# Up matrix of the feed-forward network in seven block products of Strassen's kind, tokens in two passes, the residual kept in memory

## The chip, the cores and the metric

The kernel runs on one core of a Trainium2 chip. The metric is device microseconds of one execution, lower is better. Beside its time, one profiled execution is given: the profile lists every instruction of the engines TensorE (PE, with its weight loads as PEld), VectorE (DVE), ScalarE (ACT), GpSimd (POOL) and the queue of SyncE (SP), which here only issues DMAs.

## The reference

One decoder layer on 1024 prompt tokens and 64 sample tokens (1088 in all), model width 1024. The change lies in its last step, and all ahead of it (projection, selection, sparse attention, convolution) is as before.

```python
def mix_and_mlp(x, attn_o, conv_o, w_out, g_mix_post, g_mlp_pre, w_up, w_down, g_mlp_post):
    m = jnp.einsum('bte,ed->btd', jnp.concatenate([attn_o, conv_o], axis=-1), w_out)
    x = x + rmsnorm(m, g_mix_post)
    h = rmsnorm(x, g_mlp_pre)
    f = jnp.einsum('btf,fd->btd', jnp.square(jax.nn.relu(jnp.einsum('btd,df->btf', h, w_up))), w_down)
    return x + rmsnorm(f, g_mlp_post)
```

`w_up` is 1024 x 4096, `w_down` is 4096 x 1024, all float32.

## The kernel before

Everything below is in `phase_out_mlp`, the last phase; each engine has its program in the order of the code, and semaphores are the only link between engines. Precision comes from splitting: each float32 operand is a high part (rounded to the type fp32r) and a low part (the rest), and one product of two blocks is three matmuls, high x high, high x low, low x high (`product`, L2185 to L2187). So every operand, weights too, has to be made: ACT casts the high part (L2083 for weights, L2152 for the hidden values), POOL subtracts for the low part of weights (L2030), DVE for that of the hidden values (L2336).

First come nine tiles of rows of the output projection (`out_rows`, `turn_rows`), then the feed-forward network, in `NG` = 8 groups of 4 blocks of 128 hidden channels. A group has an up part of 12 blocks (4 channel blocks x 3 token chunks of 384, 384 and 320), each 8 x 3 matmuls into one PSUM bank, and a down part of 24 blocks (8 output blocks x 3 token chunks), each 4 x 3 matmuls, whose sums DVE adds to `acc0` and `moT` in SBUF (L2355). The matmuls of both parts are as wide as the chunk. Six banks go round. ACT takes the relu (L2160), DVE squares (L2343), ACT makes the high part and DVE the low part, and a block of the down part that needs the last hidden values comes behind others that don't. Weights come as eight slices of 128 x 1024 a group (`load`, 512 KB each); a slice is made high and low once and serves all 1088 tokens. Groups 1 to 6 are a loop. At the end `final_rows` turns the sums back to rows on PE, and ACT, POOL and DVE make the last norm; the input rows plus the first residual stay in SBUF (`x2`).

## Time and profile before

| | us |
|---|---|
| three runs | 1678.77, 1668.45, 1679.35 (median 1678.77) |
| the profiled execution | 1670.35, span 1668.6 |
| PE busy | 1536.3 (92%), mean granted clock 0.967 |
| DVE, ACT, POOL busy | 705.1, 612.4, 417.9 |

The span runs from the first to the last instruction; 1.75 us of the profiled time lie around it. A busy PE in such a table is one with a matmul in flight; how fast it goes is read from the distance between the starts of neighbouring matmuls.

### The profile page before, as it was taken

How to read it: one execution, taken by the hardware profiler on the slowest of the kernel's cores; microseconds unless marked ns; L12 is line 12 of the kernel's file. 1: busy time of each engine (PE TensorE's matmuls, PEld its weight loads, DVE VectorE, ACT ScalarE, POOL GpSimd, SP SyncE). 2: the span in 40 equal slices, each digit the busy share in tenths (PEclk: the TensorE clock that was granted, in tenths of full speed). 3: DMA queues.
4: the chain of work that ended last, by engine and by line, in shares of the span. 5: the costliest groups of instructions: out<-in, count | busy, mean ns of one | idle time of the engine just before them, and what ended most of it. 6: DMA issues, size and time to landing. Idle time of an engine off the chain costs nothing.

```text
span 1668.6 us, 22157 instructions
## 1 busy us (share of the span) xinstructions
PE 1536.3 (92%) x8544; PEld 1278.9 (77%) x8544; DVE 705.1 (42%) x1322; ACT 612.4 (37%) x1092; POOL 417.9 (25%) x432
## 2 busy tenths in 40 slices
PE   3798888998979999885999999999999999999995
PEld 2356625663468877454879999999999999999995
DVE  1234916777976544246454222222222222222224
ACT  3112725888325765474433112121212212030211
POOL 2132100112594221104332212121212121212124
PEclk9999998999989998997999999999999999999998
DMA  6011104143007000337001111111111111111112
GB/s 208 19 37 24 49 11 119 60 68 67 7 3 224 36 2 1 119 134 246 0 1 51 44 46 47 43 42 46 49 39 50 38 50 38 50 38 50 39 45 101
DMA packets 92884, 97.66 MB, mean 59 GB/s; under 512 B 14822, under 2 KB 80438, under 8 KB 90500
## 3 DMA queue, kind: packets, MB, share of 16 engines
q1 hardware_dynamic: 89324, 75.71, 15.5%
q0 software_dynamic: 3488, 20.98, 3.4%
q8 instruction: 46, 0.75, 0.2%
q14 instruction: 26, 0.21, 0.0%
HBM read 85.55 MB, written 11.45 MB: 58 GB/s over the span
## 4 chain that ended last, share of the span: by engine, by line
PE 51%; DVE 1%; POOL 1%; DMA 1%; issue 0%; ACT 0%; SPq 0%; DVEq 0%; POOLq 0%; ACTq 0%
PE ps L2185 17%; PE ps L2187 17%; PE ps L2186 17%; PE ps L2219 0%; POOL y L2069 0%; DVE wo L2291 0%; DVE y L2366 0%; DMA wo_raw<-in_w_out 0%; DMA out_y_p<-y 0%; POOL wlo L2030 0%; PE ps L2271 0%; DVE xlo L2282 0%; DVE wlo L2287 0%; DVE y L2376 0%; SPq L1979 0%
## 5 line engine op out<-in xcount | busy, mean ns | idle before, releaser
L2030 POOL TENSOR_TENSOR wlo<-wraw,whi 128x1024 fp32r<-128x1024 f32 x62 | 149.0, 2403 | 573.1 <-ACT whi L2083 573.1
L2186 PE MATMUL ps<-xlo,whi 128*128 128x384 f32 (+1 forms) x768 | 250.3, 326 | 0.0
L2185 PE MATMUL ps<-hhi,whi 128*128 128x384 f32 (+1 forms) x720 | 235.1, 327 | 0.8 <-POOL wlo L2030 0.8
L2187 PE MATMUL ps<-hhi,wlo 128*128 128x384 f32 (+1 forms) x720 | 235.2, 327 | 0.0
L2186 PE MATMUL ps<-hlo,whi 128*128 128x384 f32 (+1 forms) x720 | 234.9, 326 | 0.0
L2083 ACT CAST whi<-wraw 128x1024 fp32r<-128x1024 f32 x62 | 65.2, 1052 | 296.5 <-PE ps L2187 293.8
L2343 DVE TENSOR_TENSOR rel<-rel 128x384 f32<-128x384 f32 (+1 forms) x96 | 51.5, 537 | 283.6 <-ACT rel L2160 283.6
L2186 PEld LDWEIGHTS ps<-xlo,whi 128*128 128x128 f32 x768 | 144.2, 188 | 0.0
L2160 ACT ACTIVATE rel<-ps 128x384 f32<-128x384 f32 (+1 forms) x96 | 45.3, 473 | 264.3 <-PE ps L2187 264.3
L2185 PEld LDWEIGHTS ps<-hhi,whi 128*128 128x128 f32 x720 | 135.2, 188 | 1.1 <-POOL wlo L2030 1.1
L2187 PEld LDWEIGHTS ps<-hhi,wlo 128*128 128x128 f32 x720 | 135.2, 188 | 0.0
L2186 PEld LDWEIGHTS ps<-hlo,whi 128*128 128x128 f32 x720 | 135.1, 188 | 0.0
L1040 PE MATMUL ps<-hT,w 128*128 128x384 f32 (+1 forms) x384 | 120.3, 477 | 8.6 <-DMA w<-in_w_u 8.6
L2185 PE MATMUL ps<-xhiA,whi 128*128 128x384 f32 (+1 forms) x384 | 125.7, 327 | 0.8 <-POOL wlo L2030 0.8
L2187 PE MATMUL ps<-xhiA,wlo 128*128 128x384 f32 (+1 forms) x384 | 125.4, 327 | 0.0
L2187 PE MATMUL ps<-xhiC,wlo 128*128 128x384 f32 (+1 forms) x384 | 125.1, 326 | 0.0
L2185 PE MATMUL ps<-xhiC,whi 128*128 128x384 f32 (+1 forms) x384 | 125.1, 326 | 0.0
L1040 PEld LDWEIGHTS ps<-hT,w 128*128 128x128 f32 x384 | 74.1, 194 | 53.9 <-DMA w<-in_w_u 8.7
L1115 DVE TENSOR_SCALAR_CACHE_REDUCE mask<-moT,cand 128x384 bf16<-128x384 f32 (+3 forms) x132 | 109.0, 882 | 1.1
L473 PE MATMUL ps<-w,hT 128*128 128x328 f32 (+3 forms) x256 | 97.0, 534 | 0.0
L2355 DVE TENSOR_TENSOR moT<-ps,moT 128x384 f32<-128x384 f32 (+1 forms) x84 | 45.0, 535 | 119.8 <-PE ps L2187 119.7
L2355 DVE TENSOR_TENSOR acc<-ps,acc 128x384 f32<-128x384 f32 (+1 forms) x84 | 45.0, 535 | 113.7 <-PE ps L2187 112.8
(304 smaller groups left out, 2860.8 us busy)
## 6 DMA issues: line engine op xcount, KB each, us to landing
wraw<-in_w_up SPq DMA_DIRECT2D x32, 512.0 KB, 4.0
wraw<-in_w_down SPq DMA_DIRECT2D x32, 512.0 KB, 3.4
x<-in_x SPq DMA_DIRECT2D x16, 512.0 KB, 10.0
w<-in_w_rows SPq DMA_DIRECT2D x2, 2048.0 KB, 11.3
w<-in_w_u SPq DMA_DIRECT2D x2, 2048.0 KB, 10.5
wo_raw<-in_w_out SPq DMA_DIRECT2D x8, 512.0 KB, 6.2
out_y_p<-y SPq DMA_DIRECT2D x8, 512.0 KB, 2.6
up<-by_channel SPq DMA_DIRECT2D x32, 86.0 KB, 4.0
```

The source lines that it names most:

```text
L473: last = nc.tensor.matmul(bank[2 + u % 2][0:n, 0:w], hT[:, k, i * P:i * P + n], wslot[g % 2][:, k, 0:w], start=(k == 0), stop=(k == KC - 1))
L1040: last = nc.tensor.matmul(bank[2 + 2 * (q % 3) + half][:, 0:w], wslot[c // 2][:, k, col:col + P], hT[:, k, t0:t0 + w], start=(k == 0), sto ...
L1115: last = nc.vector.tensor_scalar(mk, sc, against[0:n, j:j + 1].bitcast(F32), None, op, ALU.add, accum_out=count[0:n, j:j + 1])
L2030: nc.gpsimd.tensor_tensor(wlo_of(j, last), raw[:], whi_of(j, last), ALU.subtract).then_inc(s_wlo, 1)
L2083: nc.scalar.copy(whi_of(j, last), raw[:]).then_inc(s_whi, 1)
L2160: nc.scalar.activation(rel[:, p % 3, 0:w], bank[b % NBK][:, 0:w], ACT.Relu).then_inc(s_re, 1)
L2185: nc.tensor.matmul(o, wh, xh, start=first, stop=False)
L2186: nc.tensor.matmul(o, wh, xl, start=False, stop=False)
L2187: return nc.tensor.matmul(o, wl, xh, start=False, stop=last)
L2343: nc.vector.tensor_tensor(rel[:, p % 3, 0:w], rel[:, p % 3, 0:w], rel[:, p % 3, 0:w], ALU.mult).then_inc(s_sq, 1)
L2355: nc.vector.tensor_tensor(dst, src, dst, ALU.add).then_inc(s_ad, 1)
```

## The change

All of it is in `phase_out_mlp` (and one weight tile, `uw4`, reserved in place of `xhiA`).

- The up matrix is worked in units of 256 hidden channels (two blocks of 128) against half of the model width (4 blocks of 128) twice, and against two halves of the tokens of a pass. That is a 2 x 2 by 2 x 2 block product, made with seven block products in place of eight (a form with shared sums: four sums of weight blocks, `sums`; four of input blocks, `x_t1` to `x_t4`; seven sums of results in PSUM, SBUF and DVE). A unit is 7 x 4 x 3 = 84 matmuls, each as wide as half of a pass.
- The tokens go in two passes, of 512 (halves of 256) and 576 (halves of 288): `both_passes` runs the eight groups twice. Weights are therefore loaded, split and summed twice, and what was made once for 1088 tokens is made for 512 and again for 576.
- The seven operands of a unit (`uw`, high and low) have one place each. `up_high` (ACT) and `up_low` (POOL) refill place i once PE has done product i of the unit before. The raw slice (`uraw`, now 1 MB) has one place too: `load_up` waits until all seven low parts of the unit before are made.
- `FBANK` gives each product its bank: products 0, 3 and 5 go on top of each other in bank 0, and ACT copies what stands there in between (`take`); 4 and 6 do so in bank 3. `sum_hidden` (DVE) makes the four hidden blocks from copies and banks, `squared` is relu and square in one.
- The down part has the form of before, with chunks of 512 in the first pass and 288 in the second (384 and 192 in its last group), on three banks. For its first three chunks PE does hidden blocks 0 to 2 and comes back for block 3.
- The rows x + residual go to DRAM (`rows_d`) and come back at the end. The rows of the first pass are finished in the first group of the second.
- Preparing the inputs of a pass is seven casts (`x_high`), seven subtractions (`x_low`) and four sums of 4 x 256 or 4 x 288 elements.

```diff
+    HALF_T = (256, 288)
...
+    FBANK = [0, 1, 2, 0, 3, 0, 3]
+    OPENS = (0, 1, 2, 4)
+    SUM_AT = {2: 4, 3: 2, 4: 3, 5: 1}
+    DBANK = [4, 5, 1]
...
+    def x_source(p, i):
+        return [block(p, 0, 0), block(p, 1, 0), block(p, 1, 1), block(p, 1, 1), block(p, 0, 1), block(p, 0, 0),
+                block(p, 1, 0)][i]
...
+    def w_source(i):
+        return [quarter(0, 0), quarter(0, 1), quarter(0, 1), wsum[:, 1, :, :], quarter(1, 0), wsum[:, 0, :, :],
+                quarter(1, 1)][i]
...
+    def both_passes(eng, body):
+        for p in range(2):
+            body(p, 0, True, False)
+            with eng.Fori(1, NG - 1) as g:
+                body(p, g, False, False)
+            body(p, NG - 1, False, True)
...
+            def load_up(g, j):
+                sp.dma_start(uraw[:].rearrange("p k h n -> p k (h n)"),
+                             up[:, :, bass.ds(g * (FG * P) + j * 2 * P, 2 * P)]).then_inc(s_ru, 16)
...
+            def body(p, g, first, last):
+                if not (p == 0 and first):
+                    sp.wait_ge(s_wlo, at(p, g, 1, NP))
+                    load_up(g, 1)
+                if not (p == 1 and last):
+                    sp.wait_ge(s_wlo, at(p, g, 1, NP) + NP)
+                    load_up(after(p, g, last)[1], 0)
...
+                else:
+                    up_low(p, g, 1, range(NP))
+
+                for d in range(2):
+                    down_low(p, g, d, last)
...
+                if more:
+                    up_low(*nxt, 0, (0, 1))
+                down_low(p, g, 2, last)
+                if more:
+                    up_low(*nxt, 0, (2, 3, 4))
+                down_low(p, g, 3, last)
+                if more:
+                    up_low(*nxt, 0, (5, 6))
...
+            def up_high(p, g, j, which, unit0=False):
+                for i in which:
+                    act.wait_ge(s_ru, at(p, g, j, 16) + 16)
+                    if i in SUM_AT:
+                        act.wait_ge(s_sum, at(p, g, j, 4) + SUM_AT[i])
+                    if not unit0:
+                        act.wait_ge(s_up, at(p, g, j, NP) - NP + i + 1)
+                    nc.scalar.copy(uw_of(i, 0), w_source(i)).then_inc(s_whi, 1)
...
+            def take(p, g, j, which, start):
+                hw, slot = HALF_T[p], {0: 0, 3: 1, 4: 2, 5: 0}[which]
+                act.wait_ge(s_up, at(p, g, j, NP) + which + 1)
+                if which == 5:
+                    act.wait_ge(s_add, at(p, g, j, 4) + 1)
+                elif not start:
+                    act.wait_ge(s_add, at(p, g, j, 4) - (0 if which == 3 else 1))
+                nc.scalar.copy(pb[:, slot, 0:hw], bank[FBANK[which]][:, 0:hw]).then_inc(s_cp, 1)
...
+                take(p, g, 0, 0, start)
...
+                up_high(p, g, 1, (0, 1, 2))
+                take(p, g, 0, 3, start)
+                up_high(p, g, 1, (3,))
...
+                take(p, g, 0, 4, start)
+                up_high(p, g, 1, (4,))
+                take(p, g, 0, 5, start)
...
+                up_high(p, g, 1, (5,))
+                hid_high(p, g, 0, 0)
+                up_high(p, g, 1, (6,))
+                hid_high(p, g, 0, 1)
+
+                take(p, g, 1, 0, False)
+                down_high(p, g, 0, last)
...
+            def unit(p, g, j, first, last_):
...
+                    if i == 5:
+                        pe.wait_ge(s_cp, N_CP + n4 + 2)
+                    if i == 6:
+                        pe.wait_ge(s_cp, N_CP + n4 + 3)
+                    for k in range(HK):
+                        s = slice(k * P, (k + 1) * P)
+                        last = product(bank[FBANK[i]][:, 0:hw], (uw[i][:, 0, s], uw[i][:, 1, s]),
+                                       (moving(p, i, 0)[:, k, :], moving(p, i, 1)[:, k, :]),
+                                       k == 0 and i in OPENS, k == HK - 1)
                     last.then_inc(s_up, 1)
...
+                        if q < 3:
+                            pe.wait_ge(s_hlo, N_HLO + grp(p, g, 4) + (4 if f == 3 else 3))
...
+                for q in range(3):
+                    part(q, range(FG - 1))
+                for q in range(3):
+                    part(q, range(FG - 1, FG))
+                for q in range(3, len(todo)):
+                    part(q, range(FG))
...
+            def sums(p, g, j):
+                n4 = at(p, g, j, 4)
+                dve.wait_ge(s_ru, at(p, g, j, 16) + 16)
+                nc.vector.tensor_tensor(wsum[:, 0, :, :], quarter(1, 0), quarter(1, 1), ALU.add).then_inc(s_sum, 1)
+                dve.wait_ge(s_sum, n4 + 1)
+                nc.vector.tensor_tensor(wsum[:, 1, :, :], wsum[:, 0, :, :], quarter(0, 0), ALU.subtract).then_inc(s_sum, 1)
+                nc.vector.tensor_tensor(quarter(1, 0), quarter(0, 0), quarter(1, 0), ALU.subtract).then_inc(s_sum, 1)
+                dve.wait_ge(s_sum, n4 + 2)
+                dve.wait_ge(s_wlo, at(p, g, j, NP) + 2)
+                nc.vector.tensor_tensor(quarter(0, 1), quarter(0, 1), wsum[:, 1, :, :], ALU.subtract).then_inc(s_sum, 1)
...
+            def sum_hidden(p, g, j, which):
+                n4, n7, hw = at(p, g, j, 4), at(p, g, j, NP), HALF_T[p]
+                b = lambda i: bank[i][:, 0:hw]
+                s = lambda i: pb[:, i, 0:hw]
+                if which == 0:
+                    dve.wait_ge(s_up, n7 + 2)
+                    dve.wait_ge(s_cp, N_CP + n4 + 1)
+                    o, x, y = ct[:, 0, 0, 0:hw], b(1), s(0)
+                elif which == 1:
+                    dve.wait_ge(s_cp, N_CP + n4 + 4)
+                    o, x, y = ct[:, 0, 1, 0:hw], b(2), s(0)
+                elif which == 2:
+                    o, x, y = ct[:, 1, 1, 0:hw], s(2), s(0)
+                else:
+                    dve.wait_ge(s_up, n7 + 7)
+                    o, x, y = ct[:, 1, 0, 0:hw], b(3), s(1)
+                nc.vector.tensor_tensor(o, x, y, ALU.add).then_inc(s_add, 1)
+            def squared(p, g, j, h):
+                dve.wait_ge(s_add, at(p, g, j, 4) + 2 * (h + 1))
+                o = ct[:, h, :, 0:HALF_T[p]]
+                nc.vector.scalar_tensor_tensor(out=o, in0=o, scalar=0.0, in1=o, op0=ALU.max,
+                                               op1=ALU.mult).then_inc(s_sq, 1)
+            def hid_low(p, g, j, h):
+                hw = HALF_T[p]
...
+                sum_hidden(p, g, 0, 1)
+                squared(p, g, 0, 0)
+                sum_hidden(p, g, 0, 2)
+                hid_low(p, g, 0, 0)
+                sum_hidden(p, g, 0, 3)
+                squared(p, g, 0, 1)
...
+                    if q == 0 and not late:
+                        sums(*after(p, g, last), 0)
```

**Two places in the order of instructions.** First ACT at the head of a group in the loop. Before:

```order
L2160 ACTIVATE rel<-ps 128x384 [waits o_hlo]
L2152 CAST hhi<-rel 128x384 [waits o_sq]
...
L2160 ACTIVATE rel<-ps 128x320 [waits o_hlo,o_up]
...
L2083 CAST whi<-wraw 128x1024 [waits o_up,o_raw0]
...
L2160 ACTIVATE rel<-ps 128x384 [waits o_hlo,o_up]
L2152 CAST hhi<-rel 128x320 [waits o_sq]
```

And after the change, in the loop of the first pass; `o_sum` is the semaphore of the weight sums on DVE, `o_ru` that of the raw slice, and the line L2327 is `take`:

```order
L2327 COPY moT<-ps 128x256 [waits o_add]
...
L2228 CAST uwA<-uraw 128x512 [waits o_up,o_ru]
...
L2228 CAST uwA<-uraw 128x512 [waits o_up]
...
L2227 REGISTER_ALU [waits o_sum]
L2228 CAST uwA<-uraw 128x512 [waits o_up]
...
L2327 COPY moT<-ps 128x256 [waits o_add,o_up]
```

The copy of product 3 now stands behind three casts of weights, the third of which waits for the fourth weight sum.

Second DVE at the end of the up part and the head of the down part. Before (the first group, whose sums are copied):

```order
L2343 TENSOR_TENSOR rel<-rel 128x320 [waits o_re]
L2336 TENSOR_TENSOR hlo<-rel,hhi 128x384 [waits o_hhi]
L2336 TENSOR_TENSOR hlo<-rel,hhi 128x320 [waits o_hhi]
L2353 COPY acc<-ps 128x384 [waits o_dn] x2
L2353 COPY acc<-ps 128x320 [waits o_dn]
```

After the change (`o_wf` counts the chunks of the down part that PE has done):

```order
L2672 TENSOR_TENSOR moT<-ps,moT 128x256 [waits o_ah]
L2678 SCALAR_TENSOR_TENSOR moT<-moT 128x2x256 [waits o_add]
L2672 TENSOR_TENSOR moT<-moT 128x256
...
L2685 TENSOR_TENSOR hlo<-moT,hhi 128x512 [waits o_oh]
...
L2760 TENSOR_TENSOR moT<-ps,moT 128x512 [waits o_wf]
...
L2591 TENSOR_TENSOR moT<-uraw 128x512 [waits o_ru]
...
L2593 TENSOR_TENSOR moT<-moT,uraw 128x512 [waits o_sum]
L2594 TENSOR_TENSOR uraw<-uraw 128x4x128
...
L2597 TENSOR_TENSOR uraw<-uraw,moT 128x4x128 [waits o_wlo]
...
L2760 TENSOR_TENSOR moT<-ps,moT 128x512 [waits o_wf] x2
```

Four weight sums for the next group now stand between the first and the second addition of the down part.

On POOL a group was eight subtractions of 128x1024; it is fourteen of 128x512 and four of 128x1024 now, in each of the two passes, with the last two of the four behind low parts of the next group's up weights.

## Rows read from the trace of the kernel before

**Rows 1.** The page: busy time of the engines (share of the span) and instructions.

```profile
PE 1536.3 (92%) x8544; PEld 1278.9 (77%) x8544; DVE 705.1 (42%) x1322; ACT 612.4 (37%) x1092; POOL 417.9 (25%) x432
```

**Rows 2.** Windows: stretch, length, busy us (count) of engines, granted clock, DMA share, GB/s.

```profile
1300.00:1400.00 100.00, 100.00 (x607) 100.00 (x606) 25.69 (x50) 19.24 (x34) 20.93 (x9) 1.00 0.16 47
```

**Rows 3.** Who waited for whom from 893 to 1640 us: total, times, longest.

```profile
POOL wlo L2030 <- ACT whi L2083: 566.4, 60, 14.0
ACT rel L2160 <- PE ps L2187: 264.3, 93, 3.7
```

**Rows 4.** Timeline of PE: starts at 512 and at 384 columns.

```profile
780.60 0.39 PE L2185 MATMUL ps<-wo,xhiC 128*128 128x512 f32 x1
...
796.24 0.39 PE L2185 MATMUL ps<-wo,xhiC 128*128 128x512 f32 x1
...
1002.07 0.33 PE L2185 MATMUL ps<-xhiA,whi 128*128 128x384 f32 x1
...
1008.66 0.33 PE L2187 MATMUL ps<-xhiC,wlo 128*128 128x384 f32 x1
```

**Rows 5.** Timeline of PE in the attention, narrower matmuls.

```profile
645.29 0.28 PE L1520 MATMUL ps<-keys,qS 128*128 128x256 f32 x1
645.41 0.49 PE L1530 MATMUL ps<-identf,kpT 128*128 128x128 f32 x3
...
665.78 0.30 PE L1519 MATMUL ps<-keys,qS 128*128 128x128 f32 x1
665.92 0.28 PE L1520 MATMUL ps<-keys,qS 128*128 128x128 f32 x1
```

**Rows 6.** Groups by shape from 745 us: count, busy us, mean ns, idle before.

```profile
L2160 ACT ACTIVATE rel<-ps 128x384 f32<-128x384 f32 x64 | 31.3, 491 | 181.8 <-PE ps L2187 181.8
L2127 ACT CAST xhiA<-moT 128x512 fp32r<-128x512 f32 x8 | 4.9, 616 | 0.0
L2083 ACT CAST whi<-wraw 128x1024 fp32r<-128x1024 f32 x62 | 65.2, 1052 | 296.5 <-PE ps L2187 293.8
L2355 DVE TENSOR_TENSOR acc<-ps,acc 128x384 f32<-128x384 f32 x56 | 31.2, 557 | 79.1 <-PE ps L2187 78.2
L1369 POOL TENSOR_TENSOR qS<-qT,qS 64x512 fp32r<-64x512 f32 x12 | 15.4, 1279 | 0.9
L2030 POOL TENSOR_TENSOR wlo<-wraw,whi 128x1024 fp32r<-128x1024 f32 x62 | 149.0, 2403 | 573.1 <-ACT whi L2083 573.1
```

**Rows 7.** Timeline of ACT, DVE and POOL: start, us, engine.

```profile
811.51 0.68 DVE L2287 TENSOR_TENSOR wlo<-moT,whi 128x512 fp32r<-128x512 f32 x1
811.67 2.77 POOL L2054 TENSOR_TENSOR x<-x,moT 128x1024 f32<-128x1024 f32 x1 [1.40 <-DVE moT L2319]
812.11 2.89 DVE L2329 TENSOR_TENSOR xlo<-moT,xhiA 128x512 fp32r<-128x512 f32 x1
...
885.21 2.85 POOL L2030 TENSOR_TENSOR wlo<-wraw,whi 128x1024 fp32r<-128x1024 f32 x1
...
885.73 1.27 DVE L2312 TENSOR_TENSOR moT<-ps,gvec 128x512 f32<-128x512 f32 x2
```

**Rows 8.** Timeline: from the last matmul of an up block on.

```profile
1000.34 0.31 PE L2187 MATMUL ps<-xhiC,wlo 128*128 128x320 f32 x1
...
1000.68 0.44 ACT L2160 ACTIVATE rel<-ps 128x320 f32<-128x320 f32 x1 [2.62 <-PE ps L2187]
...
1001.15 0.49 DVE L2343 TENSOR_TENSOR rel<-rel 128x320 f32<-128x320 f32 x1 [2.43 <-ACT rel L2160]
```

**Rows 9.** DMA issues: KB each, median us from issue to landing.

```profile
moT<-by_time SPq DMA_DIRECT2D x2, 1088.0 KB, 5.3
```

**Rows 10.** Timeline of PE: work behind an idle time of 2.60 us.

```profile
687.18 1.12 PE L1618 MATMUL ps<-identf,kpage 128*128 128x128 f32 x7 [2.60 <-ACT kpT L1469]
```

**Rows 11.** Windows with the clock behind an idle PE.

```profile
688.00:694.00 6.00, 5.17 (x23) 3.96 (x21) 1.38 (x2) 2.19 (x4) 0.94 (x1) 0.50 0.53 182
```

**Rows 12.** Timeline of PE: the last matmul of the down part.

```profile
1647.37 0.31 PE L2187 MATMUL ps<-hhi,xlo 128*128 128x320 f32 x1
```

863 lines of the change are left out of this document (545 added, 318 removed).

## The prediction

> **What bounds the kernel now.** I read the page first: PE is busy 92% of the span, the others a quarter to two fifths [rows 1]. Then the windows: in the feed-forward network PE is busy 100.00 of 100 us at full clock, DVE 26, ACT 19, POOL 21 [rows 2]. Then the waits: POOL waits for ACT, ACT for PE, each for hundreds of us [rows 3], and no long wait is PE's. So this stretch, from about 878 to 1647.5 us [rows 12], is a stream of matmuls, and a matmul saved is time saved, as long as the others keep up. Last I read what the others would need: widths of matmuls, durations of ACT, DVE and POOL, and what happens when DVE and POOL meet.
>
> **Matmuls: -36 us.** In a dense stretch the distance of starts is (796.24-780.60)/69 = 0.2267 us at 512 columns and (1008.66-1002.07)/38 = 0.1734 at 384 [rows 4]: 0.0134 us plus N/2400. So 320 columns cost 0.147, 288 cost 0.1334, 256 cost 0.120; the one pair of 256 columns in the trace has 0.12 [rows 5]. Up before: 768 x (2 x 0.1734 + 0.147) = 379 us. Up after: 16 units a pass x 84 = 1344 matmuls a pass, 1344 x (0.120 + 0.1334) = 341. Down before: 379 too. Down after: 768 x 0.2267 + 1344 x 0.1334 + 96 x 0.1734 + 96 at 192 columns, for which I take 0.11: 381. Net 2 - 38 = -36. Narrow pairs of 128 columns stand 0.14 apart [rows 5], where the line says 0.067; if 256 and 288 can't go under that, the up part costs 1344 x (0.02 + 0.007) = 36 us more. The 256-column row decides for the line.
>
> The row of 0.2267 us at 512 columns and the line through it also speak on a rule of the Trainium skill (TensorE: Matmul & The Clock Gate, Back-to-back issue gap): for pairs of weight load and matmul it has about 81 ns at 128 columns and 131 at 512. By that, a matmul of 256 columns would cost nearly as much as one of 384, and 384 more of them would make the up part some 10 us longer instead of 38 shorter. The trace doesn't agree with it, so it changes neither sum nor chances.
>
> **The others' work.** Durations: ACT 384 columns from PSUM 0.49, 512 from SBUF 0.62, 1024 1.05; DVE 384 0.56; POOL 512 1.28, 1024 2.40 [rows 6]; DVE 512 with both inputs in SBUF 0.68, 512 from PSUM twice in 1.27 [rows 7]. From these: `take` of 256 0.38, `sum_hidden` 0.43. A group of the first pass is 2 x 84 x 0.120 + 96 x 0.2267 = 41.9 us on PE; POOL has 14 x 1.28 + 4 x 2.40 = 27.5, DVE some 19, ACT some 19. The throughput is there. Latency isn't, since every place (raw slice, weight operand, bank) is single.
>
> A second fact makes it worse. DVE with two SBUF inputs doesn't run beside POOL: L2329 needs 0.68 alone but began at 812.11, POOL's L2054 at 811.67, and it ended 0.55 after POOL did. POOL in turn, called while DVE's L2287 ran, took 2.77 [rows 7]. An input in PSUM isn't touched (two L2312 in 1.27 under a POOL instruction). They take turns: whoever comes second waits for the other's whole instruction. Of DVE's new work `sums`, `squared`, `hid_low` and one `sum_hidden` are of this kind, 11.7 us a group, against POOL's 27.5: the two together fill 39 of 42.
>
> **Waits of PE in a group of the first pass**, 0 being its first matmul, a product 1.44 us. Handoffs: PE's slot end to ACT 0.20, ACT to DVE 0.03 [rows 8]; to POOL 0.16 and to PE 0.15 are taken between.
>
> (A) End of the up part. The down part's first matmul waits for `hid_low` of hidden block 2. After product 5: 0.20 + `take` 0.38 + sum 0.43 + `squared` 0.68 + cast 0.62 + `hid_low` 0.68 + handoffs 0.27 = 3.26, of which product 6 covers 1.44: 1.8 us. POOL may lengthen it.
>
> (B) Product 5 of unit 0. The next raw slice is asked for once the low parts of this unit are made, 3.1 us ahead of 0 (E below); 1 MB needs 5.3 us [rows 9], so it lands at 2.2. Casts 0 and 1 end at 3.0 and 3.7, POOL's low parts run 3.2 to 4.5 and, after the first weight sum (4.5 to 5.0), to 6.2; sums 2 to 4 end at 6.7, 7.3, 7.9; cast 2 at 8.55; only then comes `take` of product 3, 8.8. PE, due at 7.2, goes on at 9.0: 1.8 us. Without meeting POOL: 0.1.
>
> (C) Product 3 of unit 1. Unit 0 ends at 11.9. `take` of its product 5 ends at 11.0; from there POOL's low parts 4, 5 and 6 alternate with `squared` (13.0), sum (14.4), `hid_low` (16.1), then sum, `squared` 17.15, cast 17.8, and behind it in ACT's queue `take` of unit 1's product 0, 18.1. PE is due at 11.9 + 4.3 = 16.2, goes on at 18.25: 2.05 us. Without meeting POOL: 0.
>
> (D) Fourth chunk boundary of the down part. PE, on three banks, needs addition 1 before chunk 4; the four weight sums stand ahead of it. Chunk 0 ends 6.8 into the down part, its addition 0.9 later, sums 1 and 2 1.3 more, then POOL's low part of down weights holds DVE for 2.3, sums 3 and 4 and the addition 1.7: 13.1 against 10.9, 2.2 us. Without POOL 0.5.
>
> (E) Weights of chunk 6. POOL makes three low parts (3.7) and then 2.4 of down weights; 45.1 against 44.5, 0.7 us with handoffs, either way. Two more low parts end at 47.5, the group at 50.7, which gives B its 3.1.
>
> Sum 1.8 + 1.8 + 2.0 + 2.2 + 0.7 = 8.6, and A in its own group is 1.95 (POOL holds the lock for 0.25 there): 8.8. Second pass, product 1.60, chunks of 288: the same steps give A 1.9, B 0.8, C 1.7, D 1.5 (a chunk is 1.6 us, so D is dear even without POOL, 1.25), E none: 5.9, and 4.4 in the last group, which has no sums. All: 8 x 8.8 + 7 x 5.9 + 4.4 = +116 us. Lower bound, never meeting POOL: 8 x 3.1 + 8 x 3.15 - 1.25 = +49.
>
> **Once each.** Start: the first group's products wait for 11 casts and subtractions of 1024 elements (1.05 to 1.22 each), half of them under the last rows of the output projection, and `take` of product 3 stands behind all: 3 to 20, I take +11. Between the passes the same 11 subtractions and sums on DVE (1.3 each, 14.6) beside additions and POOL in 22 us of down part: 5 to 20, +12. Norm of the first pass inside two units: 5 to 15, +10; PE's turning of rows only moves. Tail: 1668.6 - 1647.5 = 21.1 us now [rows 12], with three tiles of rows; two tiles later and no sum with x from POOL: 12, so -9 (-4 to -12). Loading up and down weights twice, and the rows' way through DRAM, stands at nothing: 47 GB/s now [rows 2], twice that is far from the 206 that 1088 KB in 5.3 us make. Freeing `x2` buys nothing either.
>
> **Sum.** -36 + 116 + 11 + 12 + 10 - 9 = +104. Against the profiled execution, 1670.35 us (span 1668.6 and 1.75 around it), 1774. That execution is 8 us under the median of 1678.77, and the three runs differ by 11, so this is about 1770 to 1780; I say **1775**. Less than 1%, 17 us, a measurement of this kernel can hardly tell from no change.
>
> **Rivals.**
> 1. DVE and POOL seldom meet on the path (another rhythm). For it: before, they met rarely. Against: together they fill 39 of 42 us. Then 49 in place of 116, and the single items at their low ends: -36 + 49 + 3 + 5 + 5 - 9 = +17, 1687; in between, up to 1730.
> 2. The clock. Behind an idle time of 2.60 us in the trace [rows 10] the granted clock was 0.50, the lower level, for 6 us [rows 11]. The change makes some 32 idle times of 2 us or more. If every other one is followed by 3.4 us at half clock (1.7 us lost), +27; if each, +54: 1800 to 1828.
> 3. Narrow matmuls above the line: +36 on top, partly hidden in the waits, 1800.
> 4. Faster: the waits don't reach PE. It is decided in (A) to (E): -36 over 16 groups is 2.3 us a group. Below that it is faster; fully covered it ends at -36 + 3 + 5 + 5 - 9 = -32, 1638. Against it: A alone, in which nothing can overlap, is 1.8, and D without POOL 0.5 and 1.25.
>
> That the change doesn't do what it says is excluded: the order of instructions shows 84 matmuls of 256 a unit.
>
> **Chances.** Forecast (1735 to 1795) 0.54; rival 1 0.21, of which 0.06 within 1% of before; rival 2 0.15; rival 3 0.04; rival 4 0.06. The range leaves out rival 4, the lowest of 1 and the highest of 2: 1695 to 1812. Faster by over 1% 0.05, within 0.08, slower 0.87.
>
> **In the profile after.** Starts 0.120 and 0.133 apart in the up parts prove the matmul term. PE's waits should name: hlo of DVE at the head of the down parts (A), the copies of ACT before products 3 and 5 (B, C), DVE's additions before chunk 4 (D). DVE's mean for `sums` and `squared` well over 0.68 proves the meeting with POOL, at 0.7 rival 1. PE's busy share should fall under 88% from 878 us on, and the group should repeat at about 51 and 54 us. Wrong I'd be if POOL's 512-column subtraction is much shorter than 1.28, if the slice lands in 3 us, or if the two engines don't take turns.

## The result and the profile after

The changed kernel takes 1794.43 us (median of four, 1783.06 to 1795.96) against 1677.71: 1.0695 times the time before, interval 1.0645 to 1.0746. The forecast of 1775 was 19 us low and inside its range. The profiled execution took 1783.06 us with a span of 1781.3, so 112.7 us more than the one before; all that follows is read against that. The profiled executions of this document differ by up to 12 us ahead of the feed-forward network, where most of what the change touches begins: its first matmul starts at 876.84 us here, at 875.04 in one run below and between 881.5 and 887.3 in the others, so where a few us matter the time from that matmul to the end is given beside the median.

The page and one window over the feed-forward network, columns as in [rows 1] and [rows 2]:

```profile
PE 1525.5 (86%) x8928; PEld 1220.2 (69%) x8928; DVE 941.7 (53%) x1524; ACT 740.1 (42%) x1312; POOL 721.4 (41%) x658
...
878.00:1781.00 903.00, 760.29 (x5080) 709.51 (x5078) 469.98 (x617) 292.44 (x510) 474.15 (x316) 0.97 0.26 84
```

PE does less (1525.5 us against 1536.3) in more time, and from 878 us on it is busy 84%, where [rows 2] had all of 100 us. Who waited for whom from 878 to 1781 us (total, times, longest), where PE had no long wait before [rows 3]:

```profile
POOL uwA L2129 <- ACT uwA L2228: 251.7, 54, 12.0
...
PE ps L2407 <- ACT moT L2327: 53.2, 31, 12.6
...
PE ps L2407 <- DVE hlo L2685: 28.0, 16, 3.1
...
PE ps L2407 <- DVE moT L2760: 21.9, 13, 2.1
PE ps L2407 <- POOL dwlo L2134: 12.8, 8, 8.2
...
PE ps L2448 <- ACT moT L2290: 6.0, 1, 6.0
```

L2327 is `take`, L2685 `hid_low`, L2760 the additions of the down part, L2134 the low parts of down weights: the names of (B) and (C), (A), (D) and (E). The single waits of 12.6, 8.2 and 6.0 us are no part of the repeated groups: the first and the last belong to the start (L2290 is the norm of the last 64 rows), the 8.2 to the turn from the first pass to the second. One group of the first pass (its first matmul starts at 1058.65), from the timeline of PE, the rows with an idle time ahead of them:

```profile
1067.32 0.39 PE L2407 MATMUL ps<-xb,ring 128*128 128x256 f32 x1 [1.38 <-ACT moT L2327]
1076.59 0.38 PE L2407 MATMUL ps<-xb,uwA 128*128 128x256 f32 x1 [1.87 <-ACT moT L2327]
1084.31 0.50 PE L2407 MATMUL ps<-hhi,dwhi 128*128 128x512 f32 x1 [1.80 <-DVE hlo L2685]
1097.52 0.50 PE L2407 MATMUL ps<-hhi,dwhi 128*128 128x512 f32 x1 [2.04 <-DVE moT L2760]
1103.94 0.49 PE L2407 MATMUL ps<-hhi,dwhi 128*128 128x512 f32 x1 [0.69 <-POOL dwlo L2134]
```

The same five places each time; their waits add up to 8.6 us, and steps under 0.1 us each make it 9.0. The pace is the distance of two starts in a dense stretch at the same width. A wait counts below as the distance of two starts less the pace, about 0.15 more than the idle time in the row (the modelled end of a matmul lies behind the next start). The second pass has four (the last row is from the group before the other three):

```profile
1506.59 0.40 PE L2407 MATMUL ps<-xb,ring 128*128 128x288 f32 x1 [0.55 <-ACT moT L2327]
1516.18 0.40 PE L2407 MATMUL ps<-xb,uwA 128*128 128x288 f32 x1 [1.33 <-ACT moT L2327]
1524.51 0.40 PE L2407 MATMUL ps<-hhi,dwhi 128*128 128x288 f32 x1 [1.67 <-DVE hlo L2685]
...
1478.70 0.40 PE L2407 MATMUL ps<-hhi,dwhi 128*128 128x288 f32 x1 [1.27 <-DVE moT L2760]
```

Where the time went, by the starts of PE in both traces (feed-forward network alone, 789.8 us before, 904.5 after; it began 2 us earlier):

| term | forecast | measured |
|---|---|---|
| matmuls, at the paces of the trace | -36 | -38 |
| waits (A) to (E), 16 groups | +116 | +116 (9.0 a group, then 5.7) |
| start | +11 | +24 |
| between the passes | +12 | +14 |
| norm of the first pass inside two units | +10 | +9 |
| tail | -9 | -13 |
| a piece of the lower clock level inside a group | 0 | +1 |

The start is the first up part, 53.3 us long, less 20.2 of matmuls, 5.5 of usual waits, the 2.4 of three turnings of rows of which before had two, and the 1.7 that before lost there. Between the passes: the last down part of the first pass, 36.7 less 21.8 and 3.4, and 2.8 more in the up part ahead of it. The norm: 34.1 less 22.4 and 4.2 in the first up part of the second pass, and 1.5 in its down part. The tail: the last down part and all behind it lose 14.4 us against 27.3. Of the norm and the tail 3.2 us are PE's turning of rows, which went from the one to the other and which the forecast counted in neither; without it they are 6 and -10. The terms add up to 113 of 114.7 us; the rest is one more turning at the start and rounding.

What stood behind the 8.2 us at the turn (start, us, engine):

```profile
1314.04 2.21 ACT L2251 CAST xb<-xraw 128x1152 fp32r<-128x1152 f32 x2 [7.29 <-issue]
1316.15 1.04 ACT L2239 CAST dwhi<-draw 128x1024 fp32r<-128x1024 f32 x1
1317.27 2.36 POOL L2134 TENSOR_TENSOR dwlo<-draw,dwhi 128x1024 fp32r<-128x1024 f32 x1 [4.52 <-ACT dwhi L2239]
1319.68 0.79 PE L2407 MATMUL ps<-hhi,dwhi 128*128 128x512 f32 x1 [8.19 <-POOL dwlo L2134]
```

ACT's queue has two casts of inputs for the second pass ahead of the cast of the last down weights, and the first of them came only when DVE had made its sums of inputs.

Five whole groups in one row, a window in the first pass and one in the second, columns as in [rows 2]:

```profile
1006.32:1262.48 256.16, 217.10 (x1321) 191.49 (x1320) 127.66 (x160) 83.45 (x150) 140.96 (x90) 0.99 0.26 82
1417.08:1685.71 268.63, 244.59 (x1800) 239.88 (x1800) 126.44 (x201) 85.30 (x150) 141.39 (x90) 1.00 0.25 78
```

A group takes 51.2 and 53.7 us, where its matmuls alone are 41.9 and 48.0. DVE is busy 25.5 and POOL 28.2 of the 51.2, so neither is full.

### The profile page after: what moved, and what is told of

It is laid out like the page before. It is cut to its first block, busy times and chain, and to the rows that moved or that the text cites. A ratio compares the mean times of both kernels' runs of the same rounds, so it can differ in the third digit from the quotient of the medians.

```text
span 1781.3 us, 24842 instructions
## 1 busy us (share of the span) xinstructions
PE 1525.5 (86%) x8928; PEld 1220.2 (69%) x8928; DVE 941.7 (53%) x1524; ACT 740.1 (42%) x1312; POOL 721.4 (41%) x658
## 4 chain that ended last, share of the span: by engine, by line
PE 23%; issue 13%; DVE 9%; POOL 9%; ACT 2%; DMA 1%; POOLq 0%; ACTq 0%; DVEq 0%; SPq 0%
PE ps L2407 8%; PE ps L2409 7%; PE ps L2408 7%; POOL dwlo L2134 3%; POOL uwA L2129 3%; POOL ring L2129 2%; DVE hlo L2685 1%; DVE moT L2672 1%; DVE moT L2678 1%; DVE moT L2591 1%; DVE xraw L2608 1%; ACT moT L2327 1%; DVE uraw L2597 1%; DVE xb L2601 1%; POOL uw L2129 0%
## 5 line engine op out<-in xcount | busy, mean ns | idle before, releaser
L2407 PE MATMUL ps<-hhi,dwhi 128*128 128x288 f32 (+3 forms) x736 | 247.3, 336 | 67.4 <-DVE hlo L2685 28.0
L2409 PE MATMUL ps<-hhi,dwlo 128*128 128x288 f32 (+3 forms) x736 | 243.0, 330 | 0.0
L2408 PE MATMUL ps<-hlo,dwhi 128*128 128x288 f32 (+3 forms) x736 | 243.0, 330 | 0.0
L2129 POOL TENSOR_TENSOR uwA<-uraw,uwA 128x512 fp32r<-128x512 f32 x96 | 133.0, 1399 | 253.5 <-ACT uwA L2228 253.5
L2134 POOL TENSOR_TENSOR dwlo<-draw,dwhi 128x1024 fp32r<-128x1024 f32 x62 | 151.3, 2450 | 128.2 <-ACT dwhi L2239 128.2
L2407 PEld LDWEIGHTS ps<-hhi,dwhi 128*128 128x128 f32 x736 | 139.1, 189 | 88.9 <-DVE moT L2760 23.7
L2760 DVE TENSOR_TENSOR moT<-ps,moT 128x288 f32<-128x288 f32 (+3 forms) x168 | 87.5, 533 | 202.3 <-PE ps L2409 202.3
L2407 PE MATMUL ps<-xb,uwA 128*128 128x256 f32 (+1 forms) x512 | 150.4, 294 | 27.8 <-ACT moT L2327 25.6
L2408 PE MATMUL ps<-xb,uwA 128*128 128x256 f32 (+1 forms) x512 | 149.3, 292 | 0.0
L2409 PE MATMUL ps<-xb,uwA 128*128 128x256 f32 (+1 forms) x512 | 148.7, 290 | 0.0
L2409 PEld LDWEIGHTS ps<-hhi,dwlo 128*128 128x128 f32 x736 | 139.1, 189 | 10.6
L2408 PEld LDWEIGHTS ps<-hlo,dwhi 128*128 128x128 f32 x736 | 139.2, 189 | 9.6
L2327 ACT COPY moT<-ps 128x256 f32<-128x256 f32 (+1 forms) x128 | 49.1, 384 | 220.7 <-PE ps L2409 219.8
L2407 PEld LDWEIGHTS ps<-xb,uwA 128*128 128x128 f32 x512 | 97.8, 191 | 31.9 <-ACT moT L2327 21.8
L2408 PEld LDWEIGHTS ps<-xb,uwA 128*128 128x128 f32 x512 | 97.9, 191 | 0.4
```

The lines of the kernel that those rows point to most:

```text
L2129: nc.gpsimd.tensor_tensor(uw_of(i, 1), w_source(i), uw_of(i, 0), ALU.subtract).then_inc(s_wlo, 1)
L2134: nc.gpsimd.tensor_tensor(dw_of(1, d, late), draw[d % 2][:], dw_of(0, d, late), ALU.subtract).then_inc(s_dlo, 1)
L2327: nc.scalar.copy(pb[:, slot, 0:hw], bank[FBANK[which]][:, 0:hw]).then_inc(s_cp, 1)
L2407: nc.tensor.matmul(o, wh, xh, start=first, stop=False, skip_group_check=True)
L2408: nc.tensor.matmul(o, wh, xl, start=False, stop=False, skip_group_check=True)
L2409: return nc.tensor.matmul(o, wl, xh, start=False, stop=last, skip_group_check=True)
```

## The experiments

All are changes of the changed kernel, and times are medians beside the changed kernel's 1794.4. This table holds PE's waits in a steady group of each run (us beyond the pace, read from the timeline of PE), and the mean length of five groups. "unit 0 p5" is the wait before product 5 of unit 0; "p6", "p3" likewise. "Head" is the wait before the first matmul of the down part, "chunk 4" and "chunk 6" those before these chunks of it, and "third step" one inside its first three chunks, where PE comes to the next hidden block. A "place" is the one buffer of one operand.

| run | first pass | group | second pass | group |
|---|---|---|---|---|
| changed kernel | unit 0 p5 1.54, unit 1 p3 2.03, head of down 1.95, chunk 4 2.20, chunk 6 0.85 | 51.2 | 0.71, 1.49, 1.83, chunk 4 1.42 | 53.7 |
| hidden blocks in steps | p5 1.32, p3 2.03, chunk 4 2.19 | 50.4 | 0.71, 1.49, third step 0.92, chunk 4 2.33 | 54.3 |
| take 3 first | unit 0 p6 0.75, p3 2.30, head 1.76, chunk 4 2.19, chunk 6 0.85 | 51.4 | p3 1.66, head 1.83, chunk 4 1.43 | 53.1 |
| take 0 early | p5 1.58, unit 1 p5 1.05, head 2.56, chunk 4 2.19, chunk 6 0.85 | 51.2 | p5 0.71, head 2.41, chunk 4 1.20 | 54.0 |
| sums between | p5 1.32, p3 2.01, head 1.76, chunk 4 0.98, chunk 6 3.09 | 54.6 | 0.71, 1.49, 1.83 | 52.2 |
| all four | p6 0.42, unit 1 p5 1.35, chunk 4 0.98, chunk 6 3.06 | 49.5 | unit 1 p5 0.34, third step 1.36, chunk 4 0.39 | 50.4 |
| short POOL | head 1.76 | 43.8 | head 1.84, chunk 4 1.19 | 51.1 |
| PSUM operand | head 1.76, chunk 4 0.47, chunk 6 0.57 | 45.2 | head 1.82, chunk 4 1.17 | 51.1 |
| five edits | p6 2.76, unit 1 p5 1.36, chunk 4 0.98 | 47.1 | unit 1 p5 0.63, third step 1.36, chunk 4 0.40 | 51.0 |

### One wait at a time

**Hidden blocks in steps.** The first three chunks of a down part begin with two hidden blocks.

```diff
-                            pe.wait_ge(s_hlo, N_HLO + grp(p, g, 4) + (4 if f == 3 else 3))
+                            pe.wait_ge(s_hlo, N_HLO + grp(p, g, 4) + max(f + 1, 3 if p == 1 and first else 2))
...
-                for q in range(3):
-                    part(q, range(FG - 1))
-                for q in range(3):
-                    part(q, range(FG - 1, FG))
+                for fs in ((range(3),) if p == 1 and first else (range(2), range(2, 3))) + (range(3, 4),):
+                    for q in range(3):
+                        part(q, fs)
```

> The first three chunks of a down part now begin with hidden blocks 0 and 1 alone, and come back for block 2 and then block 3, so that PE no longer needs the low part of block 2 at the head (not in the first group of the second pass, which stays). Theory, each wait stands by itself: the step of 1.95 us (first pass, 8 groups) and 1.84 us (second pass, 7 groups) between the up part and the down part goes, 8 x 1.95 + 7 x 1.84 = 28 us, so about 1766 us against 1794. Rival, the chain of weights (raw slice, sums, casts, low parts) sets the period of a group and the waits are elastic: the waits before products 5 and 3 or before chunks 4 and 6 grow by what is saved, under 10 us comes back, 1785 or more.

1783.85 us, 1.0626 times before (1.0608 to 1.0643): 10.6 us less, of 28. Both theories hold in part. In the second pass the rival does: the wait left the head and came back at the third step (0.92) and at chunk 4 (2.33 in place of 1.42). In the first pass the waits fell by 3.0 us a group, chunk 6 among them, but the group by 0.8 only. The clock took the rest: it is a second thing, beside waits that come up elsewhere, that eats what an edit gives back. Windows of this run, five groups and one piece:

```profile
1012.58:1264.79 252.21, 226.92 (x1321) 201.97 (x1320) 125.46 (x160) 83.17 (x150) 140.76 (x90) 0.94 0.26 83
1133.20:1136.60 3.40, 3.40 (x18) 3.40 (x17) 0.00 (x0) 1.17 (x3) 3.40 (x2) 0.50 0.26 83
```

The mean clock of these groups is 0.94, of those of the changed kernel 0.99. Two pieces of 3.4 us in four of the five groups and one in the other stand at the lower level, with PE busy throughout the one shown, and cost some 1.5 us each (a group with one takes 49.2 us, with two 50.7).

**Take 3 first.**

```diff
-                up_high(p, g, 1, (0, 1, 2))
+                up_high(p, g, 1, (0, 1))
                 take(p, g, 0, 3, start)
-                up_high(p, g, 1, (3,))
+                up_high(p, g, 1, (2, 3))
```

> ACT copies product 3 of unit 0 out of bank 0 before it makes the high part of place 2, which waits for the fourth weight sum. Theory, each wait by itself: the step of 1.54 us (first pass) and 0.71 (second) before product 5 goes, 8 x 1.54 + 8 x 0.71 = 18 us, to about 1776 us; the 12.8 us before product 5 in the very first unit shrink by 4 to 6, since the copy then waits for the raw slice and two casts but not for the sums. Rival, elastic waits: product 3 of unit 1 then waits longer by the same amount, since what it waits for hangs on the weight sums and POOL and not on PE, and under 7 us comes back.

1789.91 us (ratio 1.065, 1.0614 to 1.0686), not to be told from the changed kernel by its interval. In the second pass the group is 0.6 us shorter, near the 0.7 of the theory. In the first, product 6 waits 0.75 for the next `take`, now behind the same weight sum, product 3 of unit 1 waits 0.3 longer, and the clock falls more often (0.97 in five groups). The rival is nearer. In the first unit the wait before product 5 fell from 12.7 to 6.9 us, but one of 3.3 before product 6 came in its place.

**Take 0 early.**

```diff
-                hid_high(p, g, 0, 1)
-
                 take(p, g, 1, 0, False)
+                hid_high(p, g, 0, 1)
+
```

> ACT copies product 0 of unit 1 before it casts hidden block 1 of unit 0. The copy then needs the third sum of unit 0, not the squares behind it. Theory: the step of 2.03 us (first pass) and 1.50 us (second) before product 3 of unit 1 goes, 8 x 2.03 + 8 x 1.50 = 28 us, to about 1766 us. Rival: the copy comes only some 1 us earlier, because DVE's third sum is itself held up by POOL, and the rest of the wait stays: 10 to 15 us.

1796.84 us (1.067 to 1.0738): nothing came back, less than either theory had. The wait before product 3 went whole, more than the rival said, but 1.05 came before product 5 of unit 1 and the head of the down part grew to 2.56. The hidden blocks, for which the head waits, had become no earlier. In the second pass the waits fell by 0.9 us a group and the group became 0.3 longer: four of its five groups have a piece of 3.4 us at the lower clock level and take 54.3 us, the one without it 53.0.

**Sums between.** `sums` is split in its four instructions.

```diff
-                    if q == 0 and not late:
-                        sums(*after(p, g, last), 0)
+                    if q < 4 and not late:
+                        sums(*after(p, g, last), 0, (q,))
```

> The four weight sums of the next group stand behind the additions of chunks 0, 1, 2 and 3, one each, instead of all four behind the addition of chunk 0. Theory: the wait before chunk 4 (2.19 us in the first pass, 8 groups; 1.43 in the second, 7 groups) goes and no other comes: 27 us, to about 1767 us. Rival: the fourth sum comes later, with it casts 2 to 4 and the down weights of chunk 6 behind them on ACT and POOL, and the 0.85 us before chunk 6 grow to 2 to 3 us in the first pass and a wait appears in the second; then 10 us or less comes back.

1807.58 us (1.0751 to 1.0787), 13 slower. The second pass shows the theory pure (1.42 to 0, the group 53.7 to 52.2), the first the rival and worse: chunk 6 waits 3.09, for low parts of down weights that stand on POOL behind places 2 to 4, which stand on ACT behind the fourth sum. That is not the whole of the loss: the waits of a group grew by 0.6 us, the group by 3.4. The rest is the clock, which fell twice in every group of the first pass; the five of them, columns as before:

```profile
1024.32:1297.47 273.15, 231.25 (x1322) 203.23 (x1320) 121.78 (x160) 83.22 (x150) 142.77 (x90) 0.94 0.25 77
```

So each of (A) to (D) was where I had put it, and no one of them was worth its size, in part for the waits that came in their place and in part for the clock. That left the question what makes the chain long.

### POOL, its time or its turns

**Short POOL.** This leaves out most of POOL's subtractions; all else stays. (`g` is a number only in the first and the last group of a pass.)

```diff
-                    nc.gpsimd.tensor_tensor(uw_of(i, 1), w_source(i), uw_of(i, 0), ALU.subtract).then_inc(s_wlo, 1)
+                    n = P if isinstance(g, int) and g == 0 and p == 0 else 2
+                    nc.gpsimd.tensor_tensor(uw_of(i, 1)[:, :, 0:n], w_source(i)[:, :, 0:n], uw_of(i, 0)[:, :, 0:n], ALU.subtract).then_inc(s_wlo, 1)
...
+                n = FG * 2 * P if isinstance(g, int) and (g == 0 and p == 0 or late) else 8
```

> Leaves out most of POOL's subtractions: from the second group on, a low part of the up weights is made for 2 of 128 columns a block, one of the down weights for 8 of 1024 (the last group's down weights stay whole). Waits, casts, sums and matmuls are the same. Theory (DVE with two inputs in SBUF and POOL take turns): the means of DVE's weight sums, squares and low parts fall from 0.68 to 1.78 us to 0.68 each, and PE's steps in a group of the first pass fall from 1.54, 2.03, 1.95, 2.19 and 0.86 us to about 0.1, 0, 1.8, 0.5 and 0, in the second from 0.71, 1.49, 1.83 and 1.43 to 0, 0, 1.8 and 1.25: 8 x 6.2 + 8 x 2.2 = 67 us less and 5 more from the turn between the passes, about 1720 us. Rival (no turn taking; POOL's own durations stand in the chain of weights and nothing else): DVE's means stay as they are, only the steps before chunk 6 (0.86) and part of that before product 5 go, 15 us, 1779.

**PSUM operand.** Here POOL's work is whole, and in the six repeated groups of each pass DVE's second operand is whatever an unused PSUM bank holds. So it leaves out the right second operand, and only its time can be read.

```diff
+                i1 = o if isinstance(g, int) else ps[:, 6:8, 0:HALF_T[p]]
-                nc.vector.scalar_tensor_tensor(out=o, in0=o, scalar=0.0, in1=o, op0=ALU.max,
+                nc.vector.scalar_tensor_tensor(out=o, in0=o, scalar=0.0, in1=i1, op0=ALU.max,
...
```

`sums`, the third `sum_hidden` and `hid_low` are changed likewise.

> In the repeated groups (six of eight in each pass) DVE's weight sums, third sum, squares and low parts take their second operand from an unused PSUM bank, so the values are others; instructions, waits and POOL's work are the same as in the changed kernel. Theory (only DVE work with both inputs in SBUF takes turns with POOL): DVE's means fall to about 0.69 us though POOL runs its full 28 us a group; PE's steps in the first pass become about 0.5, 0, 1.8, 0.5 and 0.7 (9.0 to 3.5), in the second 0, 0, 1.8 and 1.2 (5.7 to 3.0): 6 x 5.5 + 6 x 2.7 = 49 us less, 1745 us. Rival (POOL's own durations in the chain made up what the run with short POOL work gained): the steps stay within a fifth of what they are, 1780 or more.

1703.63 us (1.0114 to 1.0175) and 1742.19 (1.0369 to 1.0423). Windows of five groups of each pass, first of the run with short POOL work:

```profile
1005.13:1224.11 218.98, 210.92 (x1321) 189.58 (x1320) 93.75 (x160) 83.24 (x150) 22.39 (x90) 1.00 0.30 96
1381.32:1636.81 255.49, 241.95 (x1802) 239.60 (x1801) 106.65 (x200) 85.86 (x150) 23.21 (x90) 1.00 0.26 82
```

and of the run with the PSUM operand:

```profile
1004.94:1230.74 225.80, 214.07 (x1321) 189.53 (x1320) 93.71 (x160) 83.72 (x150) 135.78 (x90) 1.00 0.30 93
1385.67:1641.01 255.34, 241.94 (x1800) 239.60 (x1801) 106.21 (x201) 85.87 (x150) 136.54 (x90) 1.00 0.26 82
```

The second pair is the one to read. POOL is busy 135.78 us, nearly as much as in the changed kernel (140.96), DVE 93.71 in place of 127.66 with the same 160 instructions, and the groups are 6.1 and 2.7 us shorter. With most of POOL's work left out instead, a group of the first pass is another 1.4 us shorter and one of the second no more. DVE by shape over the five groups of the first pass, in the changed kernel (1006.32 to 1262.48 us; count, busy us, mean ns)

```profile
L2685 DVE TENSOR_TENSOR hlo<-moT,hhi 128x512 fp32r<-128x512 f32 x20 | 19.2, 962 | 8.6 <-ACT hhi L2332 8.6
L2678 DVE SCALAR_TENSOR_TENSOR moT<-moT 128x512 f32<-128x512 f32 x20 | 18.1, 906 | 0.7
L2594 DVE TENSOR_TENSOR uraw<-uraw 128x512 f32<-128x512 f32 x10 | 17.8, 1780 | 0.0
L2672 DVE TENSOR_TENSOR moT<-ps,moT 128x256 f32<-128x256 f32 x30 | 12.6, 420 | 50.3 <-ACT moT L2327 39.0 <-PE ps L2409 11.3
```

and with the operand in PSUM:

```profile
L2688 DVE TENSOR_TENSOR hlo<-moT,ps 128x512 fp32r<-128x512 f32 x20 | 13.8, 688 | 10.4 <-ACT hhi L2332 10.4
L2680 DVE SCALAR_TENSOR_TENSOR moT<-moT,ps 128x512 f32<-128x512 f32 x20 | 13.7, 687 | 0.7
```

962 and 906 ns become 688 and 687, and the row that always had one input in PSUM, 420 ns, was as long as its width asks (0.43 us forecast). So it is shown that DVE and POOL take turns, and that this, not POOL's load, makes 5.8 of the 9.0 us of waits in a group of the first pass (6.1, less 0.3 for the one low piece of the clock among the changed kernel's five groups) and 2.7 of the 5.7 in the second. The Trainium skill (SBUF — State Buffer, SBUF: two separate sides) has this rule, a lock held for a whole instruction between a DVE instruction with two SBUF inputs and a GpSimd instruction that reads SBUF; the trace agrees, with 0.69 us and 0.96 for the same shape. The run with short POOL work gained 91 us, 19 more than the 72 expected, since its waits (B) to (E) in the first pass went whole, and the turn between the passes and the norm also lost less.

### Together

**All four** is the four edits of above in one kernel.

> The four edits of order of the first batch together. Those runs showed that a wait removed comes back in part: 4.0 us for chunk 3 of the second pass in place of 1.8 and 1.4, 3.1 before chunk 6 in the first. Theory, a chain longer than PE's work stands behind each group, and the waits only say where PE meets it: in the first pass the group stays over 49 us (7 or more lost), in the second over 51, 1775 to 1805 with the clock's dips. Rival, each edit lacked the others: with all four a group of the first pass loses under 4 us, of the second under 2, and the time is 1720 to 1745.

1755.03 us (1.0444 to 1.0479), 39 less than the changed kernel, where the four alone (11 and 5 less, 2 and 13 more) summed to nothing. The time lies between the two theories: the first pass (49.5) is the first one's, with 3.06 us before chunk 6 as in the run with sums between, and in the second (50.4) the edits had lacked each other.

**By pass.** The steps of hidden blocks in the first pass only, the sums between in the second only, take 3 first in both.

> Each edit only where it had gained: the hidden blocks in three steps in the first pass alone (2.0 us a group there), weight sums between the additions in the second pass alone (1.5 us a group), the copy of product 3 ahead of the third cast in both (0.5 and 0.63). Theory, these are additive where they were measured: 8 x 2.5 + 7 x 1.5 + 8 x 0.63 = 35 us less, of which new dips of the clock (1.5 us each, one or two in a group of the first pass in the run with the first edit) may take back up to 20: 1759 to 1779 us. Rival: without its two waits the second pass too shows dips of the clock or a new wait, and the time is above 1780.

1760.40 us (1.0481 to 1.0516), 34 less, so the gains were additive where they had been measured, and the clock (0.96 in five groups) took little more.

**Five edits** moves the last down weights ahead, in both queues.

```diff
                 down_low(p, g, 2, last)
-                if more:
-                    up_low(*nxt, 0, (2, 3, 4))
                 down_low(p, g, 3, last)
                 if more:
-                    up_low(*nxt, 0, (5, 6))
+                    up_low(*nxt, 0, (2, 3, 4, 5, 6))
```

> The four edits together, and the high and low parts of the last down weights moved ahead of those of places 2 to 4 of the next group, on ACT and on POOL. Theory: the 3.06 us before chunk 6 of the run with four edits were the fourth weight sum reached through two queues; they go, the rest stays (1.8 in the up part and about 1 before chunk 4 in the first pass, 2.4 in the second), and about 8 x 3 us plus a dip of the clock in each group come back: 1720 to 1730 us against 1755. Rival: places 2 to 6 of the next unit then come too late, and the next up part waits 3 us or more where it now waits 0.4: no change.

1738.75 us (1.0348 to 1.0404), 16 less than with four, between the two again: the 3.06 went, and 2.76 before product 6 came in place of 0.42. ACT and SP around the start of a group (1050.74 us) in this run:

```profile
1050.29 0.37 SPq L2053 DMA_DIRECT2D uraw<-in_w_up  x1
...
1055.65 1.14 ACT L2226 CAST uwA<-uraw 128x512 fp32r<-128x512 f32 x2 [2.84 <-DMA uraw<-in_w_up]
...
1060.60 0.62 ACT L2226 CAST uwA<-uraw 128x512 fp32r<-128x512 f32 x1 [3.53 <-DVE uraw L2599]
...
1062.06 0.38 PE L2405 MATMUL ps<-xb,ring 128*128 128x256 f32 x1 [2.60 <-ACT moT L2325]
```

The raw slice was asked for 0.4 us ahead of the group; in the changed kernel, 3.05 (1055.60 for 1058.65):

```profile
1055.60 0.37 SPq L2053 DMA_DIRECT2D uraw<-in_w_up  x1
```

It lands 5.3 us later, DVE's sums follow it, and PE stands behind ACT's next `take`. The wait changes its name with each edit; behind most of the names stands, as I read these rows, one chain, raw slice, sums, casts, low parts, which has one place for each.

**Sums after 1** puts all four sums behind the addition of chunk 1 in the first pass, with the down weights where they were.

> The edits of hidden blocks in steps, both early copies and the early places of the start; the down weights are back in their old place, and the weight sums stand, all four, behind the addition of chunk 1 in the first pass, and one each behind chunks 0 to 3 in the second. In the runs before, a fourth sum behind the addition of chunk 3 made the raw slice of the next unit 1 be asked for after that group had begun (1050.2 against 1050.7 less the 3.1 us of the changed kernel), and the step before product 6 was 2.7 us. Theory: with the fourth sum earlier the slice is back in time; in the first pass the wait before chunk 4 goes, one of 0.5 before chunk 5 comes, that before chunk 6 is about 1.5, and the up part loses 1.8: 3.9 us a group against 5.1; in the second 2.4 against 2.9: 8 x 1.2 + 8 x 0.5 = 13 us less, about 1718 us. Rival: DVE meets POOL's long subtraction of the down weights in the middle of the four sums, addition 2 comes 2 us late, and the time is that of the run before, 1728 to 1733.

1739.90 us (1.0348 to 1.0385), above both, and 9 more than the run with early places (below), from which it differs in the two orders alone. The intervals of the two overlap, but the feed-forward network alone takes 855.3 us against 847.6. Chunk 4 waits 0.47, addition 2 is not late, and the slice is back in time (product 6 waits 0.42), but chunk 6 waits 3.08 again: PE reaches it sooner than POOL makes its weights behind places 2 to 4. A group of the first pass is 48.1 us against 47.1. The two orders choose mainly where some 3 us are waited.

### The start

**Start order.** In the first group, `take` of products 3, 4 and 5 ahead of the casts of unit 1.

```diff
+                if start:
+                    for i in (3, 4, 5):
+                        take(p, g, 0, i, start)
                 up_high(p, g, 1, (0, 1, 2))
```

> In the first group alone ACT copies products 3, 4 and 5 of unit 0 before it makes the high parts of unit 1, whose slice comes late. Theory: the 12.8 us before product 5 go almost whole, but unit 1 can then not start before its weights (slice landed at 894.4, fourth sum 4.8 us later), so that 5 to 9 us of the time come back, to about 1787 us, and the low stretch of the clock at 891 to 905 us is shorter. Rival: the turning of the last 64 rows and their norm set the end of this group, and nothing comes back (within 2 us).

1795.46 us (1.0681 to 1.0719): nothing came back, as the rival has it. The wait before product 5, 12.56 us in the changed kernel, fell to 0.99 (idle times of the rows), but from the first `take` to the first down matmul it is 46.1 us against 46.0: the second slice is asked for 4.9 us after that `take` in both, and unit 1 needs it. The last link in both is the one that the rival names, PE's turning of the last 64 rows, behind which three of unit 1's seven products are left (the row is the changed kernel's):

```profile
921.50 1.11 PE L2448 MATMUL ps<-identf,moT 64*128 64x64 f32 x8 [6.01 <-ACT moT L2290]
```

With the new order that wait is 4.8 us. But the norm hangs on the slice too: its last step stands on ACT behind the high parts of hidden blocks and two casts of down weights, which come after the casts of unit 1. So the two theories name two ends of one chain.

**Early places** makes the high parts of places 5 and 6 earlier, so that the raw slice's one place is free sooner (on top of the five edits).

```diff
+            act.wait_ge(s_o, RT)
+            up_high(0, 0, 0, (5, 6), True)
             second(RT - 2)
```

> The five edits, and in the start ACT makes the high parts of places 5 and 6 as soon as the output projection ends, ahead of a norm and of four casts of inputs, so that the one raw slice is free sooner. Theory: the second slice of the start (asked for at 889 us) is asked for some 6 us earlier, and 4 to 6 us come back over the run with five edits. Rival: POOL's or DVE's other work at the start takes its place, under 1.5 us.

1730.75 us (1.0302 to 1.0387), 8 less than with five edits, with intervals that overlap; the profiled executions differ by 7.2 us ahead of all edits. What the edit is worth is read from the first group, 70.3 us against 73.9, and from the feed-forward network, 847.6 against 851.3: 3.5 to 3.7 us, a little under the theory. The second slice is asked for 7.7 us after the first up matmul, with five edits and in the changed kernel 12.2. This is the best version by its median, 64 us under the changed kernel and still 3.4% over the one before. No version tried beats the kernel before.

## Why the prediction was right

**What bounds it.** Right: the matmuls fell by what their pace says (0.119 to 0.120 us at 256 columns, 0.133 at 288, 0.227 at 512), and the time rose all the same. Rival 3 is out by the same numbers.

**Waits (A) to (E).** The steps held to 0.3 us each: 1.95, 1.54, 2.03, 2.20 and 0.85 against 1.95, 1.8, 2.05, 2.2 and 0.7, and 1.83, 0.71, 1.49, 1.42 against 1.9, 0.8, 1.7, 1.5; groups of 51.2 and 53.7 us against 51 and 54. Even the slice is asked for 3.05 us ahead of the group, where 3.1 stood. (The forecast's 8.6 adds the 2.05 of (C), which stands in the sum as 2.0.) That (A) to (D) are waits at those places is shown by the four single edits, each of which removed its own, the one before chunk 4 wholly in the second pass and to 0.98 in the first. What I hadn't said is that they aren't separate: the forecast holds for the kernel as written, and a reader who took the terms as the worth of a repair would have been wrong by more than half, and in two cases of four by all of it.

**DVE and POOL.** Right, and the largest single cause: without the turns the waits are 3.2 and 3.1 a group, against my bounds of 3.1 and 3.15. The run with the operand in PSUM tells it from rival 1: the two engines don't meet there, and the waits are rival 1's; in the changed kernel they are 9.0 and 5.7, which rules it out.

**The clock.** Rival 2 hardly came in the changed kernel: inside its groups the clock fell twice, at 1024.6 and at 1280.6 us, and otherwise at start and turn, where the matmuls begun at the lower level took 3.8 and 5.0 us more than their pace (in the first group's up part and in the last group of the first pass; these us are inside those two terms of the table). It did come in the edited kernels, though they idle less: twice a group in two of them. That it all but stayed away from the changed kernel's repeated groups was luck, as far as the runs show. Its price of 1.3 to 1.5 us a piece is near the 1.7 that I had.

**Once each.** Of the miss, 13 us lie in the start. I had taken 11 from a range of 3 to 20, and it was 24, outside it. I had priced the late casts and subtractions, and named the `take` behind them, but not the second raw slice: PE stood 12.56 us for it, from 887.5 to 900.3, with the clock at 0.50 from 891.5 to 905:

```profile
900.31 0.55 PE L2407 MATMUL ps<-xb,ring 128*128 128x256 f32 x1 [12.56 <-ACT moT L2327]
...
891.50:905.00 13.50, 4.69 (x22) 4.72 (x23) 8.38 (x10) 5.22 (x11) 6.07 (x6) 0.50 0.17 59
```

PE's idle time in this up part is 25.7 us, of which 5 are the usual waits of a group: 15.7 for `take` (the 12.56 and 3.1 more), 6.0 for the norm of the last rows, 2.3 for inputs and 1.7 at the head; the lower clock level is the 3.8 from above. The run with early places shows the slice to be part of it (3.5 us for a slice that is 4.5 us earlier); how the rest divides between the slice and the norm behind it no run shows.

Between the passes 12 was forecast and 14 measured, by another path than the one I had priced: I had DVE's subtractions and sums, and what PE waited 8.2 us for was the last down weights, which stand on ACT behind two casts of inputs, and the clock added 5.0. That the number was near is partly luck. So it is with the norm, which cost 4 us less than forecast without the turning of rows, and the tail, within 1 us without it.

All terms together are 9 us over the forecast, for the profiled execution: 1783 for 1774. The other 11 are the distance from that execution, the fastest of the four, to the median of 1794. I had laid the sum on the profiled execution before, which was itself 8 us under its median, and added 1 us for that; on the median the same sum gives 1783.

**Rival 4.** The waits reach PE by 9.0 and 5.7 us a group where 2.3 would decide. Even with most of POOL's work left out the kernel is 1.4% slower than before (1.1 to 1.8%): 1.8 us at the head of the down part and 1.2 before chunk 4 of the second pass stay, and the start is as long as it was.

## What to carry to other kernels

Fewer matmuls help a PE-bound kernel only if what feeds it keeps pace: where operand, bank and slice have one place each, count for one turn of the loop the path from a freed place to its refill over all queues, not the busy shares, which were about a half here. When DVE reads two operands from SBUF beside POOL, count the two engines' times as one's: an operand in PSUM gave 5.8 us a group, and leaving out most of POOL's work in its place only 1.4 more. And price waits together: take one out on the chip before believing that its size is its worth.
